# Another order of the delta rule's prologue on all five engines, with the gates' logarithm and rate in PSUM

## The reference

```python
qkv = silu(causal_dwconv(concat([q_b, k_b, v_b]), conv_w))          # 4 taps
g = -exp(a_log) * softplus(decay_logit + dt_bias)
beta = sigmoid(beta_logit)
...
q = l2norm(q) * dk ** -0.5;  k = l2norm(k)
G = cumsum(g)                                    # per chunk
decay = where(causal, exp(G[..., :, None] - G[..., None, :]), 0)
m = where(strict, einsum(k_beta, k) * decay, 0)
sol = triangular_solve(m + eye, rhs)             # by levels in the kernel
...                                              # q, k by exp(G), exp(G_last - G)
```

## Time and profile before

| | |
|---|---|
| median of 3 runs | 1113.65 us (1113.16 to 1116.85) |
| time of the profiled execution | 1116.95 us |
| its span, first to last instruction | 1114.8 us |
| PE busy | 1056.9 us (95%) |
| DVE, ACT, POOL busy | 681.1, 561.8, 412.9 us |
| mean granted TensorE clock | 0.987 of full speed |
| prologue of the delta rule, 667.68 to 719.60 us | 51.92 us, of which PE busy 39.54 |

### The profile page before, as it was taken

One profiled execution on the slowest core, in us unless ns is written; L12 is line 12 of the kernel. 1 busy time (PEld: TensorE's weight loads), 2 busy tenths in 40 slices (PEclk: granted clock), 3 DMA queues, 4 the chain that ended last, 5 costly groups with the idle time before them and its releaser, 6 DMA issues.

```text
span 1114.8 us, 21844 instructions
## 1 busy us (share of the span) xinstructions
PE 1056.9 (95%) x8226; PEld 963.6 (86%) x8226; DVE 681.1 (61%) x1079; ACT 561.8 (50%) x1022; POOL 412.9 (37%) x283
## 2 busy tenths in 40 slices
PE   9799999999999998899999997799999999999997
PEld 7699689999978997699999967688888889999996
DVE  3555767767666656667767654567677545544444
ACT  4445565555555555465555545334434255544442
POOL 1000233343341332233343354555645355534331
PEclk9999999999999999999999998899999999999999
DMA  8234466566534442466556432133312334536551
GB/s 332 78 126 127 146 205 191 184 193 192 184 114 133 151 151 76 153 207 193 186 186 195 166 114 95 49 105 96 96 58 77 114 104 160 154 114 222 183 177 38
DMA packets 46135, 162.27 MB, mean 146 GB/s; under 512 B 5248, under 2 KB 5504, under 8 KB 45952
## 3 DMA queue, kind: packets, MB, share of 16 engines
q1 hardware_dynamic: 44784, 156.79, 43.2%
q0 software_dynamic: 1296, 4.72, 1.3%
HBM read 160.44 MB, written 1.05 MB: 145 GB/s over the span
## 4 chain that ended last, share of the span: by engine, by line
PE 83%; DVE 8%; POOL 3%; ACT 3%; issue 2%; DMA 1%; DVEq 0%; POOLq 0%; SPq 0%; ACTq 0%
PE work L388 13%; PE work L390 13%; PE work L389 13%; PE work L1590 6%; PE acc L388 5%; PE acc L389 5%; PE acc L390 5%; PE work L2299 4%; PE work L2311 2%; PE acc L2311 2%; PE acc L1839 1%; POOL low L357 1%; PE acc L1853 1%; ACT high L346 1%; PE acc L1855 1%
## 5 line engine op out<-in xcount | busy, mean ns | idle before, releaser
L357 POOL TENSOR_TENSOR low<-raw,high 128x1024 fp32r<-128x1024 f32 x109 | 264.2, 2426 | 328.9 <-ACT high L346 328.9
L357 DVE TENSOR_TENSOR low<-raw,high 128x1024 fp32r<-128x1024 f32 (+3 forms) x183 | 272.7, 1497 | 165.3 <-ACT high L346 165.2
L346 ACT ACTIVATE high<-raw 128x1024 fp32r<-128x1024 f32 (+2 forms) x293 | 300.0, 1032 | 49.3 <-DMA raw<-in_w_out 23.5
L388 PE MATMUL work<-xh,high 128*128 128x256 f32 (+1 forms) x1032 | 292.6, 283 | 0.7 <-DVE low L357 0.7
L389 PE MATMUL work<-xl,high 128*128 128x256 f32 (+1 forms) x1032 | 289.5, 280 | 0.0
L390 PE MATMUL work<-xh,low 128*128 128x256 f32 (+1 forms) x1032 | 289.0, 280 | 0.0
L388 PEld LDWEIGHTS work<-xh,high 128*128 128x128 f32 (+1 forms) x1032 | 194.6, 189 | 7.7 <-issue 4.8
L389 PEld LDWEIGHTS work<-xl,high 128*128 128x128 f32 (+1 forms) x1032 | 194.9, 189 | 2.4 <-issue 0.7
L390 PEld LDWEIGHTS work<-xh,low 128*128 128x128 f32 (+1 forms) x1032 | 194.7, 189 | 0.2
L1113 POOL TENSOR_TENSOR h<-gelu,cv 128x256 f32<-128x256 f32 x44 | 48.8, 1109 | 200.5 <-ACT gelu L1033 106.7
L1590 PE MATMUL work<-xh,high 128*128 128x256 f32 x256 | 79.1, 309 | 9.5 <-DVE silu L1639 9.5
(11 more groups left out here) (383 smaller groups left out, 2230.0 us busy)
## 6 DMA issues: line engine op xcount, KB each, us to landing
raw<-in_w_ffn SPq DMA_DIRECT2D x132, 512.0 KB, 4.3
raw<-in_w_out SPq DMA_DIRECT2D x39, 512.0 KB, 4.2
raw<-in_w_diff SPq DMA_DIRECT2D x32, 512.0 KB, 4.1
raw<-in_w_att SPq DMA_DIRECT2D x32, 512.0 KB, 3.7
raw<-in_w_gdn SPq DMA_DIRECT2D x24, 512.0 KB, 4.0
raw<-in_w_mla SPq DMA_DIRECT2D x8, 512.0 KB, 3.5
raw<-in_w_gdnz SPq DMA_DIRECT2D x8, 512.0 KB, 3.6
raw<-in_w_mla SPq DMA_DIRECT2D x8, 384.0 KB, 3.2
```

The lines of the kernel that those rows point to most:

```text
L346: act.activation(high[k][:, 0:w], raw[k][:, 0:w], ACT.Copy).then_inc(high_done[k], 1)
L357: eng.tensor_tensor(low[k][:, 0:w], raw[k][:, 0:w], high[k][:, 0:w], ALU.subtract).then_inc(low_done[k], 1)
L388: pe.matmul(out, lhs[0], rhs[0], start=start, stop=False)
```

## The change

The change keeps what is computed and does it in another order, with five kinds of edit:

- **PE**: the gates are turned to rows between the two halves of the first block; the first v block (x=2, e=0) comes third instead of fifth; the gates' sums come ahead of block (1, 1), the rows behind it; the back turn of q and k comes between the halves of block (3, 1).
- **ACT**: beta's tanh and both exponentials come first of all, then the blocks; the logarithm follows the first two tanh; the spread of the sums (`gates_rows_act`) comes behind the decay's exponentials; the split of the first z chunk of slot 4 moves behind four other splits.
- **DVE**: the gates' input comes first; the negation and the maximum are one instruction; the first decay comes ahead of `gates_key_dve`.
- **PSUM**: the exponential of the rate and the logarithm are written to PSUM (`rate_at`, `log_at`, in bank `W[3]`) instead of SBUF, and the first `decay_dve` reads bank `A[0]` of `acc` instead of its copy `cum_all`. Products of pair 0 therefore wait for it (`e_["dd"]`).
- **POOL and SP**: POOL's splits follow ACT's new order, and SP's loads of chunk 2 of slots 0 and 1 move ahead of the load of chunk 1 of slot 4.

```diff
+    log_at, rate_at = W[3][:, TOK + 64:TOK + 80], W[3][:, TOK + 80:TOK + 96]
...
-    def gates_decay_act(act):
-        act.wait_ge(z_["dve"], 3)
+    def gates_exp_act(act):
+        act.wait_ge(z_["dve"], 2)
+        act.activation(rate_at, vcol("a_log"), ACT.Exp)
         act.activation(gate["e"][:], gate["abs"][:], ACT.Exp, scale=-1.0).then_inc(z_["act"], 1)
-        act.activation(flat(gate["ea"]), vcol("a_log"), ACT.Exp).then_inc(z_["act"], 1)
+
+    def gates_log_act(act):
         act.wait_ge(z_["act"], 3)
-        act.activation(gate["ln"][:], gate["e"][:], ACT.Ln, bias=1.0).then_inc(z_["act"], 1)
+        act.activation(log_at, flat(gate["e"]), ACT.Ln, bias=1.0).then_inc(z_["act"], 1)
...
-        dve.tensor_scalar(gate["neg"][:], gate["z"][:], -1.0, None, ALU.mult).then_inc(z_["dve"], 1)
-        dve.wait_ge(z_["dve"], 2)
-        dve.tensor_tensor(gate["abs"][:], gate["z"][:], gate["neg"][:], ALU.max).then_inc(z_["dve"], 1)
+        dve.scalar_tensor_tensor(gate["abs"][:], gate["z"][:], -1.0, gate["z"][:], ALU.mult, ALU.max).then_inc(z_["dve"], 1)
...
         if is0(j):
-            dve.wait_ge(z_["act"], 9)
-        c = cum_all[:, 4 * j:4 * j + 4, :] if isinstance(j, int) else cum_all[:, bass.ds(j * 4, 4), :]
+            dve.wait_ge(z_["pe"], 3)
+            dve.wait_ge(z_["dve"], 8)
+            c = quad(A[0])
+        else:
+            c = cum_all[:, 4 * j:4 * j + 4, :]
...
     def gdn_pe(pe):
         gates_project_pe(pe)
-        block_pe(pe, 0, 0)
+        gdn_block(pe, 0, 0, 0, 0)
         gates_turn_pe(pe)
+        gdn_block(pe, 0, 0, 0, 1)
         block_pe(pe, 1, 0)
+        block_pe(pe, 2, 0)
         block_pe(pe, 0, 1)
+        gates_sums_pe(pe)
         block_pe(pe, 1, 1)
-        gates_sums_pe(pe)
         gates_rows_pe(pe)
-        block_pe(pe, 2, 0)
         turn_pe(pe, 0)
         block_pe(pe, 3, 0)
         block_pe(pe, 2, 1)
+        gdn_block(pe, 3, 1, 0, 0)
         back_pe(pe, 0)
-        block_pe(pe, 3, 1)
+        gdn_block(pe, 3, 1, 0, 1)
         products_pe(pe, 0)
...
             for k in p.widths:
                 load(sp, p, k, 1)
-            for k in pz.widths:
-                load(sp, pz, k, 1)
+            load(sp, pz, 3, 1)
+            for k in (0, 1):
+                load(sp, p, k, 2)
+            load(sp, pz, 4, 1)
```

More of the change, by code:

```diff
@@ L1423, in build @@
     gate = {n: sb(f"gate_{n}", [P, HEADS, NT]) for n in
-            "z neg abs e ln sp ea g cum eg th beta vbeta tot bg kdx kd".split()}
+            "z abs e sp g cum eg th beta vbeta bg kdx kd".split()}
     grown_all = sb("grown_all", [P, HEADS, P])
@@ L1451, in gates_sums_pe @@
     def gates_sums_pe(pe):
-        pe.wait_ge(z_["dve"], 5)
+        pe.wait_ge(z_["dve"], 4)
         pe.matmul(sums_at[:, 0:16], cst("upper"), flat(gate["g"]), start=True, stop=True)
@@ L1493, in gates_input_dve @@
         dve.wait_ge(z_["dve"], 1)
-        dve.tensor_scalar(gate["neg"][:], gate["z"][:], -1.0, None, ALU.mult).then_inc(z_["dve"], 1)
-        dve.wait_ge(z_["dve"], 2)
-        dve.tensor_tensor(gate["abs"][:], gate["z"][:], gate["neg"][:], ALU.max).then_inc(z_["dve"], 1)
+        dve.scalar_tensor_tensor(gate["abs"][:], gate["z"][:], -1.0, gate["z"][:], ALU.mult, ALU.max).then_inc(z_["dve"], 1)
     def gates_decay_dve(dve):
[L1499 to L1502, removed]
+        dve.wait_ge(z_["act"], 4)
+        dve.scalar_tensor_tensor(flat(gate["sp"]), flat(gate["z"]), 0.0, log_at, ALU.max, ALU.add).then_inc(z_["dve"], 1)
+        dve.wait_ge(z_["dve"], 3)
+        dve.scalar_tensor_tensor(flat(gate["g"]), flat(gate["sp"]), -1.0, rate_at, ALU.mult, ALU.mult).then_inc(z_["dve"], 1)
         dve.tensor_scalar(gate["beta"][:], gate["th"][:], 1.0, 0.5, ALU.add, ALU.mult).then_inc(z_["dve"], 1)
-        dve.wait_ge(z_["dve"], 6)
+        dve.wait_ge(z_["dve"], 5)
         dve.tensor_scalar(gate["vbeta"][:], gate["beta"][:], 0.5, None, ALU.mult).then_inc(z_["dve"], 1)
@@ L1511, in gates_sums_dve @@
         dve.tensor_copy(flat(gate["cum"]), sums_at[:, 0:16]).then_inc(z_["dve"], 1)
-        dve.wait_ge(z_["dve"], 9)
+        dve.wait_ge(z_["dve"], 8)
         dve.tensor_tensor(flat(gate["kdx"]), sums_at[:, 16:32], flat(gate["cum"]), ALU.subtract).then_inc(z_["dve"], 1)
     def gates_key_dve(dve):
-        dve.wait_ge(z_["act"], 6)
+        dve.wait_ge(z_["act"], 5)
         dve.tensor_tensor(gate["bg"][:], gate["eg"][:], gate["beta"][:], ALU.mult).then_inc(z_["dve"], 1)
@@ L1578, in gdn_block @@
             if b_ == 0:
+                if x == 2:
+                    pe.wait_ge(z_["act"], 1)
                 if x == 3:
-                    pe.wait_ge(z_["dve"], 10)
+                    pe.wait_ge(z_["dve"], 9)
             elif x < 3:
@@ L1679, in products_pe @@
         if is0(j):
-            pe.wait_ge(z_["act"], 9)
+            pe.wait_ge(z_["act"], 8)
+            pe.wait_ge(e_["dd"], 1)
         for e in range(2):
@@ L1755, in scaled_keys_dve @@
         if is0(j):
-            dve.wait_ge(z_["act"], 7)
-            dve.wait_ge(z_["dve"], 11)
+            dve.wait_ge(z_["act"], 6)
+            dve.wait_ge(z_["dve"], 10)
         else:
@@ L2048, in gdn_act @@
         gates_take_act(act)
+        gates_beta_act(act)
+        gates_exp_act(act)
         block_mid_act(act, 0, 0, 0)
         block_high_act(act, split, 0, 0, 0)
-        refill(split, ph["gates"], 4, 0)
+        block_mid_act(act, 1, 0, 0)
         block_tanh_act(act, 0, 0, 0)
-        gates_beta_act(act)
-        block_mid_act(act, 1, 0, 0)
         block_high_act(act, split, 1, 0, 0)
-        gates_decay_act(act)
         block_tanh_act(act, 1, 0, 0)
[L2058 to L2061, removed]
+        gates_log_act(act)
         block_mid_act(act, 2, 0, 0)
         block_high_act(act, split, 2, 0, 0)
+        block_mid_act(act, 0, 1, 0)
+        block_tanh_act(act, 2, 0, 0)
+        block_high_act(act, split, 0, 1, 0)
+        block_tanh_act(act, 0, 1, 0)
+        gates_growth_act(act)
+        block_mid_act(act, 1, 1, 0)
+        refill(split, ph["gates"], 4, 0)
+        block_tanh_act(act, 1, 1, 0)
+        block_high_act(act, split, 1, 1, 0)
         for e in range(2):
             squares_act(act, 0, e)
-        block_tanh_act(act, 2, 0, 0)
         decay_act(act, 0)
+        gates_rows_act(act)
         z_tanh_act(act, 0, 0)
@@ L2178, in gdn_dve @@
     def gdn_dve(dve):
+        gates_input_dve(dve)
         block_taps_dve(dve, 0, 0, 0)
-        gates_input_dve(dve)
+        block_taps_dve(dve, 1, 0, 0)
         block_silu_dve(dve, 0, 0, 0)
-        block_taps_dve(dve, 1, 0, 0)
+        block_silu_dve(dve, 1, 0, 0)
         gates_decay_dve(dve)
+        block_taps_dve(dve, 2, 0, 0)
         block_taps_dve(dve, 0, 1, 0)
-        block_silu_dve(dve, 1, 0, 0)
+        gates_sums_dve(dve)
+        block_silu_dve(dve, 2, 0, 0)
+        block_silu_dve(dve, 0, 1, 0)
         block_taps_dve(dve, 1, 1, 0)
-        block_silu_dve(dve, 0, 1, 0)
-        gates_sums_dve(dve)
         block_silu_dve(dve, 1, 1, 0)
+        decay_dve(dve, 0)
         gates_key_dve(dve)
-        block_taps_dve(dve, 2, 0, 0)
-        decay_dve(dve, 0)
         squares_dve(dve, 0)
-        block_silu_dve(dve, 2, 0, 0)
         z_silu_dve(dve, 0, 0)
@@ L2251, in gdn_pool @@
         block_low_pool(split, 0, 0, 0)
+        block_low_pool(split, 1, 0, 0)
+        block_low_pool(split, 2, 0, 0)
+        block_low_pool(split, 0, 1, 0)
         refill(split, ph["gates"], 4, 0)
-        block_low_pool(split, 1, 0, 0)
-        block_low_pool(split, 0, 1, 0)
         block_low_pool(split, 1, 1, 0)
-        block_low_pool(split, 2, 0, 0)
         root_pool(pool, 0)
@@ L2762, in load_pairs @@
                     for k in (0, 1):
-                        load(sp, p, k, c)
+                        if c > 2:
+                            load(sp, p, k, c)
                 if j + 2 < PAIRS:
```

2 lines of the change are left out of this document (1 added, 1 removed).

## The result

Five runs of the changed kernel have a median of 1104.57 us (1102.55 to 1107.46), beside 1115.82 us (1113.16 to 1117.92) for the kernel before; the ratio is 0.9902 (0.9889 to 0.9916). That is 10.9 us less by the ratio, and 11.25 between the two medians. The forecast was 1103.4.

A forecast was written before the change was run, and what follows sets the result against it. The prediction took the chain from `root` to the levels, not PE, to bound the prologue: `root` 10.3 us earlier, the 17.10 us behind it fixed, so 1113.65 - 10.3 = 1103.35 us; range 1100.0 to 1108.0.

The forecast's parts named there:

- No wait of PE up to the end of the second v block: PE in the prologue: no wait from 667.7 until about 693, with the clock near 1.00.
- The narrow margins: PE's slack for silu: half a us before block (0,1), 0.2 to 0.4 before the turn of q and k.
- Rows of the sums: PE's turn of the gates' sums to rows: to end at 686.6 instead of 692.7, 6.1 us earlier.
- one clamp held about 2.1: DVE's `dec_l` and `dec_u`, 0.43 each bare: one held about 2.1 us by POOL's second split, `dec_u` ending at 690.5.
- `root`: DVE step behind sum of squares and mean, opening the last chain: to start at 692.2, not 702.50, 10.3 us earlier.
- The remaining chain: From `root` through masks, POOL split, load of v's chunk 2 and `mt` to the levels: fixed at 17.10 us.
- The new wait for z: PE waits 2.2 us for z's silu before block (3,1), some 1.4 us of slow clock behind it, at no cost.
- Sum: Whole kernel: 10.3 us less, 1113.65 to 1103.35 us against the median.
- Rival 1: `dec_l` and `dec_u` aren't held by POOL: `root` at 690.3, 12.2 us gained, 1101.4 us; chance 0.17.
- if the load came earlier, PE would be next: Before `mt`: the load allows it at 706.4; without that limit PE's turned mask product would set it, at 704.5.
- `bm`'s new operand: First decay on DVE read from PSUM: no wait for ACT's copy (1.88) and `grown_all` (1.02), no POOL hold, 0.69 long.

The follow-up runs named there:

- e9: The changed kernel run again unchanged: median 1105.32 us over six runs, ratio 0.9906 to the kernel before, prologue 42.4 us.
- e1: The changed kernel with ACT's tanh of the first z block ahead of `gates_rows_act`: prologue 40.8 us, pairs 163.2.
- e3: The changed kernel with the first decay's subtraction and clamp fused, eight instructions read straight from PSUM: prologue 40.2 us, pairs 162.0.
- e4: e3 with `gate_bg` also moved behind `norm_dve`: prologue 40.6 us, pairs 162.0.
- e2: The changed kernel with SP's load of v's chunk 2 moved ahead of slot 3's load of z's chunk 2: prologue 41.3 us, pairs 162.0.
- e6: The changed kernel with old operands: logarithm and rate in SBUF, first decay from `cum_all`, `gates_rows_act` before ACT's squares; maximum still one instruction: prologue 42.1 us.
- e8: e2 with POOL's split of z in slot 4 also waiting until the start of the levels is done: prologue 39.5 us, pairs 160.6.
- e10: The changed kernel with e1, e4 and e8 together: median 1096.39 us, ratio 0.9836 to the kernel before, prologue 35.2 us.
- e11: e10 without the two useless matmuls before the turn of the mask product: median 1097.48 us, ratio 0.9844 to the kernel before, prologue 35.2.

## Why the prediction was right

Point by point, in us after the first block's start, forecast against measured:

- **No wait of PE up to the end of the second v block**: right, 24.7 us without a break, at 1.00. The narrow margins held, the one before the turn of q and k with 0.2 us (silu done at 683.99, turn at 684.16).
- **Rows of the sums** ready at 18.9: `bm` started at 18.8 (684.37 less 665.61). Right.
- **`bm` 0.69, one clamp held about 2.1**: 0.69, and 2.62 for 0.42, so 2.2, plus 0.2 on the other. Right, and the step that decided the size; without this hold, the forecast would have been 12.2 us of gain.
- **`root`** at 24.5 (692.2 less 667.68): 24.2. The remaining chain, 17.10: 17.18. That this fits so closely is in part luck: the load in it took 4.99 us here and 4.86 before, and 6.08 in e9, where the same program's prologue was 42.4, only 9.5 us shorter than before.
- **The new wait for z**, 2.2: 2.2. That it costs the prologue nothing is shown by e1. The half block behind it took 2.7 us (2.8 counted), but the back turn 1.2 (695.67 to 696.86), where 0.8 was counted.
- **Sum**: 10.3 forecast, 10.6 in the prologue, 10.9 by the ratio. The prologue's own is the one to set beside the forecast; what the whole time has beyond it is within the scatter of the stretches that the change leaves alone.

Two of the prediction's statements on what lay beside the forecast were wrong. Rival 1 said that without a hold on the clamps `root` would come 1.9 us earlier. e3 shows that `gate_bg`, next in DVE's list, takes the hold, and that only 0.6 comes of it; with `gate_bg` moved as well (e4) the 1.8 is there. And "if the load came earlier, PE would be next": PE was next for `mt`, at the time given (704.5, so 36.8 us after the first block, and 36.8 in e2), but not for the levels, where POOL's hold on `inv` came in its place. The prediction also gives `bm`'s new operand 2.9 us of waits saved, beside the order; taken alone it is worth 0.8 at `root` (e6), for the hold behind it swallows the rest. What it left out is that a wait before the levels can have a price in pair 0.

## What to carry to other kernels

When POOL is busy in a row, ask of each DVE instruction beside it whether it reads SBUF twice or scales SBUF to SBUF, and follow the hold to the next such instruction before counting a gain: a hold taken off one lands on the next until none is left before POOL's row of work ends. Follow the chain that ended last, not the engine with the waits: PE lost three waits here and gained one without cost, while moving one load in SP's list was worth 1.9 us, and only with a POOL split held back that would have started 0.04 us too soon. Where the end of a stage is a wait of PE, look for its price in the next stage as well.

## What the runs showed of the hardware

- The load of 512 KB in the chain, always issued 0.37 us behind another of the same size, took from 4.5 to 6.1 us until ACT could use it, in nine traces in which this pair of loads stands alike (4.99 and 6.08 for the same program). For this reason the prologue in one trace is good to about a us.
- A DVE instruction that waits for POOL starts when POOL's current instruction ends, but the next one, even with no wait in between, finds POOL's next instruction ahead of it (0.65 and then 2.62; 0.65 to 0.67 and 2.62 to 2.63 in the five traces that have this pair of clamps under three splits). The rule of the Trainium skill, "SBUF — State Buffer", section "Who interferes with whom", that the pair is an exclusive lock held for the whole instruction, agrees with every such row: 1.86 and 2.58 us held, and `tensor_reduce` 1.21 us under a running split, its bare time.
- What a wait of PE before the levels costs in the pairs doesn't follow from its length alone. After 0.6 to 1.4 us (e8, e10, e11) the clock was 1.00 in the next 4.5 us and the pairs took 160.5 or 160.6. After 2.7 to 2.9 us it was 0.62 to 0.65, and the pairs took 161.8 to 162.0. After 4.8 and 5.2 us (e1, e6) it was 0.50, and they took 163.2. But e3, e4 and e9 waited 4.7, 4.4 and 4.4 us: e3 and e4 had 0.62 and 162.0, e9 0.50 and 162.6. What parts them stays open.
